# Mixer attention rounds: both projection blocks in a row, then turning, values and the next scores, in place of one block on either side of the turning

## What is computed

```python
def second_block(x, ...):
    h = x
    for l in range(2):
        h = h + hybrid_mixer(rmsnorm_2(h, norm_mix[l]), w_in[l], ...)
        h = h + expert_choice_ffn(rmsnorm_2(h, norm_ffn[l]), ...)   # 16 experts, 3 x 4 MB of weights each
    return rmsnorm_2(h, norm_final)

def hybrid_mixer(h, w_in, w_branch_a, w_branch_b, b_gate, sink_logit, w_out):
    proj = h @ w_in
    qa, ka, va, qw, kw, vw, gates = jnp.split(proj, SPLITS, axis=-1)
    oa = dilated_mixture(qa, ka, va)                       # 12 sub-heads
    ob, _ = banded_attention(qw, kw, vw, ..., sink_logit)  # 16 heads, window of 128 on either side
    g = sigmoid(gates + b_gate)
    return (g[:, :, 0] * (oa @ w_branch_a) + g[:, :, 1] * (ob @ w_branch_b)) @ w_out
```

## Time and profile before

| | before |
|---|---|
| median of 3 runs | 1806.93 us (1806.0 to 1807.1) |
| the profiled execution | 1806.43 us |
| its span in the profile | 1804.6 us |
| TensorE busy, share of the span | 1543.4 us, 86% |
| VectorE, ScalarE, GpSimd busy | 796.8, 588.9, 77.7 us |
| memory read | 564.18 MB |

### The profile page before, as it was taken

The page is one execution under the profiler, slowest core; times in us unless marked ns, Lnnn a source line. Parts: engine busy times, 40 slices in busy tenths (PEclk is TensorE's granted clock), DMA queues, the critical chain, the costliest instruction groups (busy, mean ns, idle before and its releaser), DMA issues.

```text
span 1804.6 us, 33023 instructions
## 1 busy us (share of the span) xinstructions
PE 1543.4 (86%) x14738; PEld 1155.0 (64%) x14738; DVE 796.8 (44%) x1634; ACT 588.9 (33%) x1049; POOL 77.7 (4%) x88
## 2 busy tenths in 40 slices
PE   9999999999999999977666666999999967656565
PEld 8989998999898888533333323798796533323232
DVE  7886678887567866210101100658764201101011
ACT  6765546665454654000000000545642000000001
POOL 1030001000003101000000000001010000000000
PEclk9999999999999999987878888999999988898887
DMA  6534446545473578999999999854589999999997
GB/s 252 199 144 159 169 165 230 206 177 192 163 280 121 208 285 359 417 430 429 431 430 429 430 430 429 351 203 148 200 343 419 429 430 430 429 430 430 430 430 311
DMA packets 46413, 567.38 MB, mean 314 GB/s; under 512 B 6736, under 2 KB 7280, under 8 KB 11328
## 3 DMA queue, kind: packets, MB, share of 16 engines
q1 hardware_dynamic: 40912, 552.50, 74.7%
q0 software_dynamic: 3744, 12.03, 1.9%
q10 hardware_dynamic: 1616, 0.74, 0.1%
HBM read 564.18 MB, written 1.05 MB: 313 GB/s over the span
## 4 chain that ended last, share of the span: by engine, by line
PE 61%; DMA 35%; another core or an unknown queue 2%; DVE 1%; SPq 0%; ACT 0%; issue 0%; DVEq 0%
DMA slab<-in_slabs 35%; PE bank L622 10%; PE bank L624 10%; PE bank L623 10%; PE bank L687 8%; PE bank L1198 4%; PE bank L688 4%; PE bank L1250 3%; PE bank L1010 1%; PE bank L1268 1%; PE bank L1069 1%; PE bank L1033 1%; PE bank L1175 1%; PE bank L574 1%; PE bank L1257 0%
## 5 line engine op out<-in xcount | busy, mean ns | idle before, releaser
L1198 PE MATMUL bank<-slab,xe 128*32 128x256 f32 x4096 | 312.1, 460 | 153.3 <-DMA slab<-in_slabs 153.2
L1290 DVE TENSOR_TENSOR wl<-slab,wh 128x1024 fp32r<-128x1024 f32 (+1 forms) x286 | 345.0, 1219 | 137.1 <-ACT wh L1991 137.1
L1991 ACT ACTIVATE wh<-slab 128x1024 fp32r<-128x1024 f32 (+1 forms) x286 | 295.6, 1044 | 183.4 <-PE bank L624 142.8
L1198 PEld LDWEIGHTS bank<-slab,xe 128*32 128x32 f32 x4096 | 142.6, 127 | 303.0 <-DMA slab<-in_slabs 193.6
L622 PE MATMUL bank<-ht,wh 128*128 128x256 f32 x768 | 219.9, 286 | 0.7 <-DVE wl L1290 0.7
L623 PE MATMUL bank<-ht,wh 128*128 128x256 f32 x768 | 217.3, 283 | 0.0
L624 PE MATMUL bank<-ht,wl 128*128 128x256 f32 x768 | 217.2, 283 | 0.0
L687 PE MATMUL bank<-ht,wh 128*128 128x512 f32 x576 | 209.5, 405 | 0.0
L1250 PE MATMUL bank<-slab,ha 128*32 128x256 f32 x2048 | 143.6, 430 | 73.6 <-DMA slab<-in_slabs 71.1
L2404 ACT ACTIVATE ta<-bank 128x256 f32<-128x256 f32 x32 | 12.3, 384 | 505.7 <-PE bank L1198 505.7
L688 PE MATMUL bank<-ht,wl 128*128 128x256 f32 x576 | 161.4, 280 | 0.0
(11 more groups left out here) (391 smaller groups left out, 2357.3 us busy)
## 6 DMA issues: line engine op xcount, KB each, us to landing
slab<-in_slabs SPq DMA_DIRECT2D x250, 2048.0 KB, 47.9
slab<-in_slabs SPq DMA_DIRECT2D x22, 1024.0 KB, 10.0
bias<-in_bias POOLq DMA_DIRECT2D x32, 192.0 KB, 3.2
slab<-in_slabs SPq DMA_DIRECT2D x6, 512.0 KB, 28.1
bias<-in_bias POOLq DMA_DIRECT2D x8, 256.0 KB, 6.8
x<-in_x SPq DMA_DIRECT2D x2, 512.0 KB, 4.5
rg<-in_rg POOLq DMA_DIRECT2D x1, 1024.0 KB, 12.3
bt<-in_rel POOLq DMA_DIRECT2D x1, 768.0 KB, 5.8
```

The source lines that it names most:

```text
L1198: t = e.matmul(bk[bank][32 * j:32 * j + 32, 0:256], XE[:, c, :], w[:, k, 256 * j:256 * j + 256], start=(c == 0), stop=(c == 7))
L1290: e.tensor_tensor(lo, src, hi.bitcast(F32), ALU.subtract).then_inc(*dve_l.mark(p))
L1991: e.activation(hi, src, ACT.Copy).then_inc(*act_h.mark(p))
```

## The change

The order of the letters in a round of the mixers' list: the first block and the second now stand side by side, and the turning follows them, directly before the values.

```diff
     sched_f = schedule(8, 32, "ffstfwv", lambda s: 3 * (s + 1))
     fills_f = [[first["fq", 0] + k] for k in range(32)]
-    sched_l = schedule(12, 28, "swftfv", lambda s: 2 * (s + 1))
+    sched_l = schedule(12, 28, "swfftv", lambda s: 2 * (s + 1))
```

## The result

| | before | after |
|---|---|---|
| median of 20 runs each | 1806.71 us | 1809.14 us (1807.51 to 1812.34) |
| ratio | | 1.0014, 95% interval 1.0008 to 1.0021 |
| span of the profiled execution | 1804.6 us | 1806.4 us |
| attention, first mixer (first scores to merge) | 120.86 us | 122.37 us |
| attention, second mixer | 120.85 us | 122.30 us |

The change costs 2.4 us, 0.14%: a small loss that twenty runs make out, and less than the 0.2% within which I call a time unchanged. The forecast was 1809.3. Two executions of the kernel before, in the later comparisons, took 1992.01 and 2399.19 us at a mean granted clock of 0.73 and 0.56 (0.93 in the others); the ratios leave them out, and are not simply the quotients of the medians.

A forecast was written before the change was run, and what follows sets the result against it. TensorE bounds the attention, loads the experts, with the merge setting the loads' start. Seams 0.6, block 24 0 and the list's end 0.6 make 1.2 us per mixer, +2.4 in all: 1809.3 us, range 1806.0 to 1814.0.

The forecast's parts named there:

- What bounds the kernel: TensorE bounds the mixers' attention, loads the experts; the merge starts the loads' stretch, so attention delays reach the end whole.
- The rival of hidden loads: Loads behind the merge take up the mixers' delay, so the time stays at 1806.9 us; chance 0.06.
- The seam of turning into values, 0.97: On TensorE, values' first matmul starts 0.97 us behind the turning's first; a round costs 0.05 us more.
- the first rival: Values behind turning wait for a full drain, 1.03 to 1.25 us; over +3.6 us in total; chance 0.28.
- Twelve rounds at 0.05: TensorE's seams cost 0.05 us in each of twelve rounds with the turning moved: +0.6 us a mixer.
- The helpers' loop, 9.0: VectorE and ScalarE's loop, maximum to maximum, grows from 8.82 to about 9.0 us.
- Block 24 waits 0: In round 12, piece 24 is ready at 643.3 and TensorE wants it at 643.36: just in time, 0 us.
- Values 11 wait 0.6: At the list's end TensorE waits 0.6 us for ScalarE's copies of turning 11, and the merge waits too.
- Sum 1.2 a mixer: Seams 0.6, block 24 0 and values 11 0.6 us make 1.2 us per mixer, +2.4 for both.
- Side by side wins: Turning to values costs 0.87 us and TensorE never waits: -1.2 us, 1805.7 us; chance 0.12.
- second and third rival: Blocks side by side win, 1805.7 us, chance 0.12; loads take up the delay, 1806.9 us, chance 0.06.
- The rival of a falling clock: In attention, TensorE's block behind 3 us without a block runs at half rate: +68 us, 1875; chance 0.02.

The follow-up runs named there:

- the delay of 9.0 us: 20 small extra TensorE products ahead of each mixer's merge, against the kernel before: 1815.3 against 1807.37 us, ratio 1.0048.
- the second comparison: The changed kernel run once more against the kernel before, on one chip: 1810.58 against 1806.83 us, ratio 1.0018.

## Why the prediction was right

Point by point, by its own steps:

- **What bounds the kernel.** Right, and now shown: the delay of 9.0 us came through as 8.7 by the ratio (7.9 by the medians), and SyncE's loads behind the merge moved with it. The rival of hidden loads falls.
- **The seam of turning into values, 0.97.** Right: 0.97 and 0.96 in the window rounds. The second block of a row takes 2.82 (2.83 forecast), and the round is 8.80 as forecast. The costlier seam of the first rival didn't come. One reading behind it was wrong: the other seams in the earlier trace rows don't all lie 0.2 behind a last start. The turning hands over to a block 0.79 - 0.76 = 0.03 behind its last start, so 0.87 was no lower bound for whatever follows a turning. The Trainium skill's rule in "TensorEngine Tiling (Array Packing)", section Tiling Modes, that a change of tiling mode drains TensorE, agrees with both: the seam without such a change is the 0.03, and the one with it, from turning to values, is 0.97 - 0.76 = 0.21.
- **Twelve rounds at 0.05.** Too high: 0.39 in place of 0.6. The four rounds of the dilated mixture cost 0.01 together, and the run with the new order in these rounds alone agrees.
- **The helpers' loop, 9.0.** Right up to the result: tanh 6.90 behind the maximum (6.89 forecast), copies 7.32 (7.29), result 8.27 (8.24). VectorE took the result up at 8.76 in place of 8.65, since it began 0.10 behind ScalarE's end where I had counted 0.04. The average of the loop is 9.04.
- **Block 24 waits 0.** This is the step that was mis-sized: it waited 0.44. The forecast had block 24 free to start at 643.34 and wanted at 643.36. Taking off the 0.99 us by which this execution's attention began later, it started at 643.60 and was wanted at 643.16. Of the 0.26 on the one side 0.2 is the loop, five times 0.04 over the 9.0 I used. The 0.2 on the other is the early rounds' seams, which I had counted and which weren't there. Two sums within 0.02 of each other were a balance of small terms. A wait can't fall below nothing, so an error of that balance can only add to it, and "just in time" should have been priced above 0.
- **Values 11 wait 0.6.** Right in size, 0.68, and in mechanism: the old order of the last turning alone takes it away.
- **Sum 1.2 a mixer.** 1.51 and 1.45 measured, so +3.0 us where +2.4 was forecast. The measured medians lie at +2.4 and, in the second comparison, +3.75. Both intervals (0.08% to 0.21%, 0.08% to 0.27%) hold 3.0 us, which is 0.17%. That 1809.14 came within 0.2 us of the forecast is in part luck: the seams were 0.2 too high, block 24 0.44 too low and values 11 0.1 too low, which leaves 0.3 a mixer missing, and the first comparison's medians happened to lie 0.6 under what the stretches give.
- **Side by side wins.** The saving exists, but the change pays it back: the second block of a row is 2.82 in place of 2.96, and turning to what follows is 0.96 in place of 0.79. The whole is a loss, so the rival falls. An order with the turning in front of both blocks does gain, in its early and its last rounds.
- **The chances.** Forecast, second and third rival add up to 0.68 within 0.2%, not 0.67.
- **The clock.** TensorE's granted clock was 1.00 throughout the changed attention (in the window 620 to 640, busy 20.00 of 20 us; over 539 to 662 it was 1.00 too). The rival of a falling clock didn't come.

How the whole splits is not a sum of two halves. TensorE's order alone costs 0.45, the helpers' alone 2.60, both together 1.51. VectorE's list and ScalarE's weren't changed one without the other, so which of them makes the helpers' part isn't shown. Each engine's list is good or bad only against the other's: with TensorE in the new order the turning comes later and its copies may wait; with TensorE in the old one the same wait is pure loss.

## What to carry to other kernels

When engines walk one list, a new order is a new order on each of their queues. Go around the loop that the helpers make among themselves, and see which step now waits for something that it didn't need before. An engine with no gap can already be served by a loop that is longer than its round (here 8.82 against 8.75). A small excess in each round piles up unseen and is paid at one place, where a round has less to do. And the end of a list has no next block to hide behind: read its last two rounds by themselves.

## What the runs showed of the hardware that was not expected

- The stretch from the first mixer's merge to the second mixer's first scores, mostly bound by loads, took 532.4 to 534.8 us over ten profiled executions, with no relation to the order in the mixers that I can see (the kernel before 534.6, the changed one 532.8 and 534.2, the known delay 532.6). The stretch from the second merge to the end took 489.7 to 492.4 us. That is why one execution's time can't tell these kernels apart, while the attention, which no load bounds, is good to 0.1 us.
- In the changed attention three waits of 0.33 us of TensorE's weight loads cost nothing, and the fourth, of 0.83, came with an idle time of 0.38 before the matmul; only the timeline of the matmuls says which one counts.
- A turning hands over to a block 0.03 us behind its last matmul's start, and to values about 0.2 behind it.
